# One start phase in place of two: modulation as 128x32 column tiles in three places, and a norm that streams single k tiles

## What is computed, as far as it matters here

```python
def _rmsnorm(x, g):
    y = xf * lax.rsqrt(jnp.mean(xf * xf, axis=-1, keepdims=True) + EPS)
    return (y * g).astype(x.dtype)
def _modulate(x, shift, scale):
    return x * (1 + scale) + shift
# per layer l, for latent tokens (c) and for context tokens (c_ctx):
mods = silu(c) @ ada_w[l] + ada_b[l]      # 1024 -> 6 * 1024: shift, scale, gate; shift, scale, gate
# even layer: u = _modulate(_rmsnorm(x), shift, scale);  z = u @ w_in
# z[:, :768] -> pooling mixer, z[:, 768:] -> 2-D Fourier mixer
```

## Time and profile before

| | |
|---|---|
| median of three runs | 4143.37 us |
| the profiled execution, its own time | 4142.88 us |
| its span | 4140.8 us |
| setup phase (0 to 187.9 us of the span) | 187.9 us |
| norm of the second phase (187.9 to about 243 us) | 55.1 us |
| products of the second phase (to 357.9 us) | 114.9 us |
| pool and Fourier phase (to about 490 us) | 132.1 us |

### The profile page before, as it was taken

The page is one execution under the profiler, slowest core; times in us unless marked ns, Lnnn a source line. Parts: engine busy times, 40 slices in busy tenths (PEclk is TensorE's granted clock), DMA queues, the critical chain, the costliest instruction groups (busy, mean ns, idle before and its releaser), DMA issues. The chain is left out here.

```text
span 4140.8 us, 69430 instructions
## 1 busy us (share of the span) xinstructions
PE 3599.3 (87%) x30916; PEld 2902.7 (70%) x30916; DVE 1640.0 (40%) x2210; ACT 671.2 (16%) x962; POOL 1005.0 (24%) x570
## 2 busy tenths in 40 slices
PE   9979897999999998799779595967778779999998
PEld 1366476788888887688668483856658667787877
DVE  0034115434344334312434555455465343434343
ACT  0121103010100010211222232222132021100000
POOL 0130123322222322432110111101021334343432
PEclk9989997999999999799889696978879879999999
DMA  8601100111111110122110101010100201111111
GB/s 321 234 26 73 56 26 21 41 41 36 36 36 31 41 36 21 56 80 72 39 44 0 49 4 44 4 45 3 40 8 3 87 31 51 46 46 46 51 41 66
DMA packets 46534, 210.59 MB, mean 51 GB/s; under 512 B 5953, under 2 KB 7489, under 8 KB 41921
## 3 DMA queue, kind: packets, MB, share of 16 engines
q1 hardware_dynamic: 42240, 189.84, 13.3%
q10 hardware_dynamic: 4032, 16.65, 1.0%
HBM read 185.63 MB, written 20.84 MB: 50 GB/s over the span
## 5 line engine op out<-in xcount | busy, mean ns | idle before, releaser
L173 PE MATMUL ps<-u_hi,w_hi 128*128 128x512 f32 (+1 forms) x2712 | 738.9, 372 | 85.9 <-DVE u_lo L404 40.8
L151 POOL TENSOR_TENSOR w_hi<-w_raw,zero 128x1024 fp32r<-128x1024 f32 x176 | 337.6, 1918 | 1645.0 <-PE ps L173 1428.8
L173 PE MATMUL ps<-u_lo,w_hi 128*128 128x512 f32 (+1 forms) x2712 | 735.7, 371 | 0.0
L173 PE MATMUL ps<-u_hi,w_lo 128*128 128x512 f32 (+1 forms) x2712 | 735.2, 370 | 0.0
L173 PEld LDWEIGHTS ps<-u_hi,w_hi 128*128 128x128 f32 x2712 | 474.3, 190 | 180.9 <-DVE u_lo L404 41.9
L173 PEld LDWEIGHTS ps<-u_hi,w_lo 128*128 128x128 f32 x2712 | 474.4, 189 | 90.3
L173 PEld LDWEIGHTS ps<-u_lo,w_hi 128*128 128x128 f32 x2712 | 474.4, 189 | 90.3
L491 DVE SCALAR_TENSOR_TENSOR ffn_cv<-ps,small,ffn_cv 128x1023 f32<-128x1023 f32 (+1 forms) x132 | 134.1, 1016 | 804.4 <-ACT ffn_cv L625 802.9
L433 DVE SCALAR_TENSOR_TENSOR h<-ps,mod,h 128x1024 f32<-128x1024 f32 (+1 forms) x288 | 282.7, 1013 | 411.7 <-PE ps L173 411.7
L154 POOL TENSOR_TENSOR w_lo<-w_raw,w_hi 128x1024 fp32r<-128x1024 f32 x176 | 425.1, 2415 | 13.8
L625 ACT ACTIVATE ffn_cv<-ps,small 128x1280 f32<-128x1280 f32 (+1 forms) x88 | 107.8, 1225 | 1319.2 <-PE ps L173 1319.2
(11 more groups left out here) (266 smaller groups left out, 4280.5 us busy)
## 6 DMA issues: line engine op xcount, KB each, us to landing
w_raw<-in_ffn SPq DMA_DIRECT2D x132, 512.0 KB, 3.4
ada_ring<-in_ada SPq DMA_DIRECT2D x24, 2048.0 KB, 7.8
w_raw<-in_cd_in SPq DMA_DIRECT2D x20, 512.0 KB, 3.9
z_scratch<-cd_stage ACTq DMA_DIRECT2D x15, 640.0 KB, 5.2
dft_tab<-in_dft_tok SPq DMA_DIRECT2D x8, 1024.0 KB, 4.8
h<-in_x SPq DMA_DIRECT2D x8, 640.0 KB, 12.6
w_raw<-in_ab_in SPq DMA_DIRECT2D x8, 512.0 KB, 3.3
w_raw<-in_ab_out SPq DMA_DIRECT2D x8, 512.0 KB, 3.3
```

Of the source, the lines that this page charges most:

```text
L151: pool.tensor_tensor(K.whi[:, slot, :], K.raw[:, raw, :], K.zero[:, 0:1].to_broadcast([P, KT * P]), ALU.add).then_inc(self.hi_done, 1)
L173: mm = pe.matmul(K.ps[:, slot, c, 0:width], wt[:, s, w], x[:, k, at:at + width], start=start and n == 0, stop=stop and n == 2)
```

## The change

The modulation is cut into 6 quads of 2048 output columns, and each quad into 16 pieces of 512 KB: piece n holds rows of k tile n // 2 and 1024 of the columns. A piece is two float32 products with 32 weight columns (two conditioning columns and 30 zeros) and 512 moving columns; the four products of a k tile go to PSUM partitions 0, 32, 64 and 96, so each sits in another 32-column strip of the array. One ACT copy and four 128x128 transposes turn a quad, one DVE instruction adds the bias.

`start_phase` takes the place of `setup_phase` and `ab_in_phase`. The input and quad 0 are loaded first. The norm `NormStream` makes its sums over k while the input arrives, then works on chunks of 512, 512 and 256 tokens and single k tiles, in a ring of 4. TensorE does tiles m = 0 and 1 chunk by chunk, waiting for each k tile, then m = 2 to 7 as before. Quads 1 and 2 are done in bursts of 3 or 5 pieces between these products, quads 3 to 5 in bursts inside `pool_fourier_phase`. There the PQ tiles get 3 banks in place of 4.

```diff
+def ada_piece(pe, K, bank, piece, n):
+    k, jj = n // 2, n % 2
+    for i in range(2):
+        j = 2 * jj + i
+        mm = pe.matmul(bank[32 * j:32 * j + 32, :], K.cond[:, k, :], piece[:, i * 512:(i + 1) * 512],
+                       start=k == 0, stop=k == KT - 1)
+    return mm
+def ada_turn(pe, K, bank, row):
+    for b in range(4):
+        mm = pe.transpose(bank[:, b * P:(b + 1) * P], row[:, b * P:(b + 1) * P], K.eye[:, :])
+    return mm
+class NormStream:
+    CHUNKS = [(0, 512, 0), (512, 512, 0), (1024, 256, 1)]
+    POOL_KS = (2, 4, 6)
+    RING = 4
...
+    def dve_scale(self, dve, c, k):
...
+        dve.wait_ge(self.spread, c + 1)
...
+        dve.scalar_tensor_tensor(self.t[:, i % self.RING, 0:w], self.K.h[:, k, at:at + w], self.gain(c, k),
+                                 self.bank(c)[:, 0:w], ALU.mult, ALU.mult).then_inc(self.scaled, 1)
+    def act_hi(self, act, c, k):
...
+        act.activation(self.K.uhi[:, k, at:at + w], self.t[:, i % self.RING, 0:w], ACT.Identity,
+                       bias=self.shift(c, k)).then_inc(self.hi, 1)
+        if k in self.POOL_KS:
+            q = self.pooled(c, k)
+            if q >= 2:
+                act.wait_ge(self.lo_pool, q - 1)
+            act.activation(self.u[:, q % 2, 0:w], self.t[:, i % self.RING, 0:w], ACT.Identity,
+                           bias=self.shift(c, k)).then_inc(self.u_out, 1)
+    def dve_lo(self, dve, c, k):
...
+        dve.scalar_tensor_tensor(self.K.ulo[:, k, at:at + w], self.t[:, i % self.RING, 0:w], self.shift(c, k),
+                                 self.K.uhi[:, k, at:at + w], ALU.add, ALU.subtract).then_inc(self.lo_dve, 1)
+    def pool_lo(self, pool, c, k):
...
+        pool.tensor_tensor(self.K.ulo[:, k, at:at + w], self.u[:, q % 2, 0:w], self.K.uhi[:, k, at:at + w],
+                           ALU.subtract).then_inc(self.lo_pool, 1)
+def start_phase(K):
...
+        @block.sync
...
+            for k in range(KT):
+                sp.dma_start(K.h[:, k, :], a["x"][k]).then_inc(x_in[k], 16)
+            for k in range(KT):
+                for jj in range(2):
+                    sp.dma_start(first[:, 2 * k + jj, :], a["ada"][0, 2 * k + jj]).then_inc(first_in[k], 16)
+                if k < 2:
+                    sp.dma_start(K.raw[:, k, :], a["ab_in"][k]).then_inc(W.loaded[k], 16)
+            for n in range(RING):
+                sp.dma_start(piece_of(n), a["ada"][1 + n // 16, n % 16]).then_inc(piece_in[n % RING], 16)
+            for b in range(2, KT):
+                sp.wait_ge(W.split, b - 1)
+                sp.dma_start(K.raw[:, b % 2, :], a["ab_in"][b]).then_inc(W.loaded[b % 2], 16)
+            for n in range(RING, 32):
+                sp.wait_ge(piece_used, n - RING + 1)
+                sp.dma_start(piece_of(n), a["ada"][1 + n // 16, n % 16]).then_inc(piece_in[n % RING], 16)
...
+        @block.gpsimd
...
+            for n in range(3):
+                W.divide_one(pool, n % 2, n % 3, n, n // 2)
+            for c in range(3):
+                for k in norm.POOL_KS:
+                    norm.pool_lo(pool, c, k)
+            for n in range(3, KT):
+                pool.wait_ge(done, n - 2)
+                W.divide_one(pool, n % 2, n % 3, n, n // 2)
...
+    RING = 5
...
+    bursts = {(1, 7): 5, (2, 7): 5, (3, 3): 3, (3, 7): 3, (4, 7): 5, (5, 7): 5, (6, 3): 3, (6, 7): 3}
+            for c, (at, w, _) in enumerate(norm.CHUNKS):
+                for m in range(2):
+                    for k in range(KT):
+                        if m == 0:
+                            norm.pe_ready(pe, c, k)
+                        mm = product_at(pe, K, m, m, K.uhi, K.ulo, k, k, c, at, w, k == 0, k == KT - 1)
+                        if (c, m, k) == (1, 0, 5):
+                            norm.pe_spread(pe, 2)
...
+            n = burst(0, bursts[1, 7])
+            for m in range(2, KT):
+                for k in range(KT):
+                    mm = product(pe, K, m % 2, m % 3, K.uhi, K.ulo, k, k, COLS, k == 0, k == KT - 1)
+                    ...
+                    if (m, k) in bursts:
+                        n = burst(n, bursts[m, k])
...
             for t in range(NT // P):
-                if t >= 4:
-                    pe.wait_ge(pq_out, t - 3)
+                if t >= 3:
+                    pe.wait_ge(pq_out, t - 2)
+                if t == 5:
+                    used = burst(used, 4)
...
+            used = burst(used, 4)
             for t in range(TT):
...
+                if t == 4:
+                    turn(3, K.ps[:, 1, 2, :])
+                used = burst(used, 2)
...
+            used = burst(used, 5)
...
+                    if m == 1:
+                        turn(4, K.ps[:, 0, 3, :])
+                    used = burst(used, 4 if m == 5 else 3)
 ...
-    nc = bacc.Bacc("TRN2", target_bir_lowering=False, num_devices=1)
+    nc = bacc.Bacc("TRN2", target_bir_lowering=False, num_devices=1, dynamic_dma_scratch_size=256)
```

More of the change, by code:

```diff
@@ L181, in bank_cols @@
     return K.ps[:, slot, :, :].rearrange("p b c -> p (b c)")[:, 0:n]
-def setup_phase(K):
-    nc, a = K.nc, K.a
[L188 to L196, removed]
+ADA_PIECES = 16
@@ L232, in _ @@
+            act.wait_ge(zeroed, 3)
+            for m in range(KT):
+                evict(m)
+                if m == 3:
+                    act.wait_ge(piece_used, 16)
+                    act.copy(row2[:, :], K.ps[:, 0, 3, :]).then_inc(row_out, 1)
+                if m == 6:
+                    act.wait_ge(piece_used, 32)
+                    act.copy(row2[:, :], K.ps[:, 0, 3, :]).then_inc(row_out, 1)
         @block.tensor
         def _(pe):
[L234 to L242, removed]
@@ L254, in _ @@
-            turn(NCH - 1)
+            pe.wait_ge(consts, 5)
+            norm.pe_sums(pe, 0)
+            norm.pe_sums(pe, 1)
+            norm.pe_spread(pe, 0)
+            norm.pe_spread(pe, 1)
+            pe.wait_ge(silu_done, 1)
+            for n in range(ADA_PIECES):
+                pe.wait_ge(first_in[n // 2], 32)
+                mm = ada_piece(pe, K, K.ps[:, 0, 0, :], first[:, n, :], n)
+            mm.then_inc(rows_done, 1)
+            pe.wait_ge(row_out, 1)
+            ada_turn(pe, K, K.ps[:, 0, 1, :], row).then_inc(turned, 1)
@@ new lines, in burst @@
+            def burst(n, size):
+                for i in range(n, n + size):
+                    pe.wait_ge(piece_in[i % RING], 16 * (i // RING + 1))
+                    mm = ada_piece(pe, K, K.ps[:, 0, 3, :], piece_of(i), i % 16)
+                    mm.then_inc(piece_used, 1)
+                return n + size
+            for c, (at, w, _) in enumerate(norm.CHUNKS):
+                for m in range(2):
+                    pe.wait_ge(W.split, m + 1)
+                    for k in range(KT):
[4 more added lines that the diff above has]
+                            norm.pe_spread(pe, 2)
+                    if c == 2:
+                        mm.then_inc(done, 1)
+                    if (c, m) == (0, 0):
+                        norm.pe_sums(pe, 2)
@@ L256, in _ @@
+            assert n == 32
         @block.vector
         def _(dve):
-            dve.wait_ge(small_in, 16)
[L259 to L268, removed]
@@ L269, in _ @@
-            dve.tensor_tensor(K.eye2[:, :], K.eye[:, 0:64], K.eye[:, 64:128], ALU.add).then_inc(gains, 1)
[L270 to L276, removed]
+            for m in range(1, KT):
+                norm.dve_acc(dve, m)
@@ new lines, in _ @@
+            dve.wait_ge(norm.lo_pool, norm.pooled(3, 0))
+            dve.wait_ge(norm.lo_dve, norm.by_dve(3, 0))
+            dve.memset(K.za[:, :, 0:8], 0.0).then_inc(zeroed, 1)
+            dve.memset(K.za[:, :, 8 + SEQ:24 + SEQ], 0.0).then_inc(zeroed, 1)
+            dve.memset(K.za[:, :, 24 + SEQ + CTX:PW], 0.0).then_inc(zeroed, 1)
+            dve.tensor_tensor(K.eye2[:, :], K.eye[:, 0:64], K.eye[:, 64:128], ALU.add).then_inc(gains, 1)
+            for quad in (1, 2):
+                dve.wait_ge(turned, quad + 1)
+                ada_mods(dve, K, K.ps[:, 1, 3, :], quad).then_inc(mod_done, 1)
@@ L670, in _ @@
             schedule(up, down, dve)
[L673 to L719, removed]
 def pool_fourier_phase(K):
@@ L753, in _ @@
             sp.dma_start(pmat[:, :, :], a["pool_w"]).then_inc(pmat_in, 16)
+            for n in range(4, RING + 4):
+                piece(n)
+            n = RING + 4
             for t in range(2, TT):
@@ L756, in _ @@
                 sp.dma_start(tab[:, t % 2, :, :], a["dft_tok"][t]).then_inc(tab_in[t % 2], 16)
+                for i in range(n, n + 2):
+                    piece(i)
+                n += 2
+            for i in range(n, 48):
+                piece(i)
         @block.tensor
```

260 lines of the change are left out of this document (232 added, 28 removed).

## The result

The changed kernel takes 4015.41 us, the median of four runs (4011.85 to 4019.28), against 4147.39 us (4141.29 to 4153.35, four runs) before: a ratio of 0.9682, 95% interval 0.9661 to 0.9703, or 132 us less. The prediction said 4010 us, 133 us less than the execution that it was worked out from. The same kernel measured twice more, on other occasions, gave 0.9685 and 0.9693. One execution of a kernel further down, early and late together, took 4932.72 us at a granted clock of 0.667; it counts in that kernel's median but not in its ratio.

What follows compares the result with a forecast made beforehand. TensorE was taken as the limit in setup, products and most of the pool phase, and as waiting throughout the norm. 4142.9 - 156.0 (start phase) + 23.3 (pool phase) = 4010 us, range 3985 to 4065.

Steps and rivals of the forecast that it cites:

- The strips: Modulation pieces: products in four different 32-column strips run at once, 0.43 us per piece; chance 0.62.
- the alternatives at 4040 and 4112 us: Modulation pieces: two strips at a time, 0.86 us per piece, chance 0.20; no overlap, 1.71 us, chance 0.12.
- The bound that spoke against four: Argument for two strips: four 64x64 tiles stream only two full depths of data, so full-depth strips may stop at two.
- 0.43 us per piece: Price of each two-product piece with four strips at once; 27 pieces outside the second burst cost 11.6 us.
- The charge for the change of tile shape: Bursts between products: about 0.3 us each, 2.4 us in the start phase; 0.2 each, 3.4 us in the pool phase.
- The pool phase: Pool and Fourier phase: 48 pieces 20.6 us, gap -2.2, three turns 1.5, 17 bursts 3.4; together +23.3 us.
- The new start: Start up to the first product: loads until T = 38.4 us, first k tile at T + 6.5, chunk 0's last about T + 20.
- T: Landing of quad 0's last piece: 38.4 us, from 14.95 MB at 424 GB/s; 46 at 350 GB/s.
- POOL behind block 2: Chunk 0: POOL splits late-landing weight block 2 before its first lo, from T + 7.4 to T + 12; k = 2 ready at T + 13.
- The stalled burst: Second burst, behind m = 2: its loads wait for the split of weight block 5; 16.7 us, with a gap of about 12.
- tiles 0 and 1: TensorE's first two m tiles, done chunk by chunk: end at T + 46, bounds T + 42 to T + 52.
- The slow rival: Loads of all pieces fall, for instance by the smaller DMA scratch, making the kernel slower than before; chance 0.02.

Runs made afterwards that it cites:

- early and late together: Changed kernel with SyncE issuing pieces 5 to 12 earlier and POOL splitting weight block 2 between its chunk 1 and 2 work: 3996.22 us, ratio 0.9641.
- the even bursts: Changed kernel with the same 80 pieces in bursts of 4 and 2 in place of 5 and 3: 4015.44 us, ratio 0.968.
- the early pieces: Changed kernel with SyncE issuing pieces 5 to 9 ahead of weight block 5 and 10 to 12 ahead of block 7: 4007.28 us, ratio 0.9662.

## Why the prediction was right

**The strips.** The prediction took four at a time from rows of 64x64 tiles, with 0.62, and the alternatives at 4040 and 4112 us. Built on purpose, they measured 4036.9 and 4109.5. So the choice between the cases was the right one. Of the two prices the one for a single strip was near: 94 us above the changed kernel (98 by the ratios) where 102 was said. The one for two strips was too high: 21 us (24 by the ratios) where 30 was said. An odd piece costs 0.86 us with four strips already, so with two it costs nothing more. That the total for two still came within 4 us is in part luck, as 4010 was 5 us too low. The bound that spoke against four, two full depths of data at a time, does not hold here: four strips of 128 rows start within 20 ns.

The Trainium skill's model for packed products (TensorE: Matmul & The Clock Gate, Part 3) gives a round the time of one product plus about 4 ns per tile. The trace here agrees in form but has about 7 ns per tile, with 20 ns between the first records of the first and the fourth product of a round. Four strips took the time of one here, more than the 3.07 times that it reports for four row tiles. Its rule there that weight loads overlap only across row groups would have cost 25 us by the prediction's count. The bursts show no such time: four strips side by side need 0.43 to 0.46 us from one record to the next, as a single product of 128 weight columns does in the earlier trace rows (0.43), and in the burst at 256.5 us the weight loads for the second records start 0.03 us behind the first records.

**A piece that was mis-sized.** 0.43 us per piece holds for pieces in pairs. An odd one costs a full 0.86, as the even bursts show. The prediction charged 27 pieces 11.6 us; the seven bursts with them are all odd, which makes 3 us more. The charge for the change of tile shape, 0.3 us per burst, was right there: from 156.15 to 173.12 us lie one m tile (24 products at 0.587 us, 14.1) and five pieces (three times 0.86 us, 2.6), which leaves 0.3.

**The pool phase,** +21.5 us measured for +23.3, came near by luck; several errors cancel. The five visible bursts with an odd piece cost 2.2 us more. A change of shape costs 0.3 us here as well and not 0.2 (a DFT step with its two pieces takes 8.06 us: 16 records at 0.43, 0.86 for the pieces, 0.33 left), 1.4 us more over the bursts that are not hidden. The last burst and the last turn cost nothing, 2.2 us less: some 5 us pass from the last pooled product to the next phase, before the change with nothing in between as well as after it. And one gain was overlooked. In the kernel before, TensorE's idle 5.2 us ahead of the pooled tiles are followed by products at half clock:

```profile
451.92 10.50 PE L806 MATMUL ps<-za,pool_mats 128*128 128x512 f32 x20 [5.17 <-ACT mix_y L828]
```
```profile
451.90:457.20 5.30, 5.28 (x8) 2.54 (x9) 2.23 (x2) 0.00 (x0) 0.00 (x0) 0.50 0.00 0
```

In the changed kernel the five pieces fill half of that gap, and the clock stays up:

```profile
315.21 4.54 PE L1093 MATMUL ps<-za,pool_mats 128*128 128x512 f32 x12 [2.48 <-ACT mix_y L1128]
```
```profile
315.20:320.00 4.80, 4.79 (x16) 2.33 (x20) 2.22 (x2) 0.22 (x1) 0.00 (x0) 1.00 0.78 312
```

The pooled products take 33.1 us before; at full clock they are 30.1 us, so 3.0 us went with the clock. The gain is not the same in every execution: in the two repetitions of the changed kernel the clock over the next 5 us is 0.66 and 1.7 us are lost, while products earlier in the phase run at a higher clock. The sum, 23.3 + 2.2 + 1.4 - 2.2 - 3.0, is 21.7.

**The new start.** T, the landing of quad 0's last piece, was taken as 38.4 us; it ended TensorE's wait at 40.2. The loads ran at 407 GB/s from 3 to 40 us and not at 424, which is 1.4 of the 1.8 us. First k tile: T + 6.5 predicted, T + 7.2 measured. POOL behind block 2: split predicted from T + 7.4 to T + 12, measured from T + 8.5 to T + 13.1, the wait at k = 2 as foretold. Chunk 0's last k tile: ready at T + 20 predicted, at T + 18 measured (DVE's instruction of 56.43 us is its last). From 55.1 us on it was no longer DVE or POOL that set the pace but TensorE itself. Behind its waits it ran at half clock, 0.43 us from record to record until 61 us and 0.23 from there, and it ended chunk 0 of m = 0 at T + 22. The 2.5 us that the prediction charged to m = 1 for a low clock fell there. So the end came out, T + 46 predicted and 86.6 us or T + 46.4 measured, with two parts of the way to it exchanged. That the split caused the wait and the long DVE instructions is shown by moving it.

**The stalled burst.** 16.7 us predicted, 17.1 measured (103.5 to 120.6 us), and shown by the early pieces: 13.7 us go with the wait. Its inside was foretold less well: a gap of about 12 us was to show it, and there are two, of 9.4 and 1.0 us, with more time in the products behind them, at a granted clock of 0.50 from 113 to 117 us.

**The sum.** Start phase 201.9 us predicted; to the same point it took 207.5, 5.6 more: 1.8 from T, 0.4 from tiles 0 and 1, 3.0 from the odd pieces and 0.4 from the stall. The pool phase took 1.8 less. Together 3.8 us, of the 5.4 by which 4015.4 lies above 4010; the rest is inside the scatter of the last stage, which in the profiled execution alone (4018.9 us) makes 5.3.

**The slow rival,** loads held up by the smaller scratch, had 0.02; it costs nothing.

## What to carry to other kernels

A float32 product cost its moving columns here, 0.43 us per record of 512, with 2, 32 or 128 weight columns alike. If only a few result rows are wanted, put several products into different 32-column strips and issue whole rounds of four, since a part of a round costs a full one. When work is scattered into bursts between other work, read each queue in order and ask what must have happened before the burst's loads can even be issued: here TensorE stood idle for 9.4 us because the refill of an empty ring stood behind a weight block that waited for the very tile before the burst. When you fill a gap, price the clock behind it too: up to 3.0 us here. An edit worth a few microseconds is read in the stages of a trace, not in the whole time, when the untouched rest scatters by 10.

## What was not expected of the hardware

An odd piece costs a whole round: 12 records in 1.9 us, and 16 records in 1.9 us. Stretches of the same 3650 us of code took from 3649.8 to 3660.5 us in different executions. DVE's instruction with both operands in SBUF took 0.74 us alone and up to 1.63 beside POOL, while the one with an operand in PSUM stayed at 0.74.
